# Keys and values of the attention heads: four full products replaced by seven block products

## What is computed

```python
h = rmsnorm(x, mix_norm_g[l])
u = h @ w_in[l]
ml_qk, ml_v, ml_o, ml_i, ml_f, mb_q, mb_k, mb_v = jnp.split(u, splits, axis=-1)
...
q_b = rmsnorm(heads(mb_q, Hb), q_norm_g[l]) * scale
k_b = rmsnorm(heads(mb_k, Hb), k_norm_g[l])
v_b = heads(mb_v, Hb)
h_b = moba_attention(q_b, k_b, v_b)
...
x = x + concat(h_m, h_b) @ w_out[l]
x = x + moe_ffn(rmsnorm(x, ffn_norm_g[l]), ...)        # 32 experts, 4 per token
x = x + sigmoid(rmsnorm(x) @ w_ple_gate[l]) * (p[l] @ w_ple_proj[l])
```

## Time and profile before

| | |
|---|---|
| Median of 3 runs | 1095.73 us (1095.69 to 1096.56) |
| Profiled execution, its own time | 1097.34 us |
| Span of the profiled execution, first to last instruction | 1095.5 us |
| Mean granted clock of TensorE | 0.995 |
| TensorE matmul busy | 1063.8 us (97%) |
| VectorE, ScalarE, GpSimd busy | 284.6, 146.9, 45.6 us |
| Bytes moved | 431.88 MB, mean 394 GB/s |

### The profile page before, as it was taken

One profiled execution on the slowest core, in us unless ns is written; L12 is line 12 of the kernel. 1 busy time (PEld: TensorE's weight loads), 2 busy tenths in 40 slices (PEclk: granted clock), 3 DMA queues, 4 the chain that ended last, 5 costly groups with the idle time before them and its releaser, 6 DMA issues.

```text
span 1095.5 us, 11997 instructions
## 1 busy us (share of the span) xinstructions
PE 1063.8 (97%) x5118; PEld 445.2 (41%) x5118; DVE 284.6 (26%) x547; ACT 146.9 (13%) x291; POOL 45.6 (4%) x59
## 2 busy tenths in 40 slices
PE   9999999999999999999998999898989899999998
PEld 5485563434343434343433333333333243534335
DVE  4286441232121212121211111121112011211126
ACT  4134350100000000000000000000000110000014
POOL 2422400000000000000000000000000000000000
PEclk9999999999999999999999999999999999999999
DMA  9942779999999999999999999999999999999991
GB/s 348 364 176 105 305 327 425 427 407 430 427 427 435 429 431 430 433 429 429 434 429 434 429 430 430 433 433 430 427 434 427 432 431 430 433 429 424 423 372 42
DMA packets 33788, 431.88 MB, mean 394 GB/s; under 512 B 5207, under 2 KB 5727, under 8 KB 16582
## 3 DMA queue, kind: packets, MB, share of 16 engines
q1 hardware_dynamic: 33520, 431.06, 93.4%
q10 hardware_dynamic: 214, 0.04, 0.0%
HBM read 430.04 MB, written 1.06 MB: 394 GB/s over the span
## 4 chain that ended last, share of the span: by engine, by line
PE 69%; DMA 29%; DVE 1%; issue 0%; ACT 0%; DVEq 0%; ACTq 0%
PE hu L1258 25%; DMA ring<-in_w_gate_up 23%; PE po L1288 15%; DMA ring<-in_w_down 6%; PE aux L1201 6%; PE hu L1053 3%; PE aux L1209 3%; PE hu L844 3%; PE hu L1250 2%; PE hu L850 2%; PE hu L887 1%; PE aux L1465 1%; PE hu L1080 1%; PE hu L860 1%; PE po L1265 1%; PE aux L1234 1%
## 5 line engine op out<-in xcount | busy, mean ns | idle before, releaser
L1258 PE MATMUL hu<-ring,num_xg 128*64 128x512 f32 x1920 | 435.3, 600 | 18.0 <-DMA ring<-in_w_gate_up 17.6
L1258 PEld LDWEIGHTS hu<-ring,num_xg 128*64 128x64 f32 x1920 | 131.9, 137 | 301.7 <-issue 271.3
L1288 PE MATMUL po<-ring,arena 128*64 128x512 f32 x976 | 217.5, 597 | 6.7 <-DMA ring<-in_w_down 6.7
L1880 DVE TENSOR_SCALAR arena<-hu 128x512 f32<-128x512 f32 x31 | 21.4, 692 | 427.8 <-PE hu L1258 427.8
L1288 PEld LDWEIGHTS po<-ring,arena 128*64 128x64 f32 x976 | 70.0, 138 | 149.3 <-issue 145.6
L1856 DVE TENSOR_TENSOR arena<-arena,aux 128x512 f32<-128x512 f32 x58 | 37.3, 684 | 133.1 <-PE aux L1209 121.3
L1201 PEld LDWEIGHTS aux<-num_xg,big 128*128 128x128 f32 x512 | 58.4, 192 | 13.0 <-issue 13.0
L1201 PE MATMUL aux<-num_xg,big 128*128 128x128 f32 x512 | 61.4, 278 | 0.0
L1869 DVE TENSOR_SCALAR arena<-iota_s,posm,gates 128x128 f32<-128x128 f32 x64 | 17.8, 342 | 118.3 <-PE po L1288 115.3
L2240 ACT ACTIVATE hu<-arena 128x512 f32<-128x512 f32 x31 | 18.6, 602 | 196.4 <-DVE arena L1880 196.4
L2256 ACT COPY arena<-po 128x512 f32<-128x512 f32 x16 | 9.4, 586 | 221.8 <-PE po L1278 221.8
(11 more groups left out here) (315 smaller groups left out, 707.6 us busy)
## 6 DMA issues: line engine op xcount, KB each, us to landing
ring<-in_w_gate_up SPq DMA_DIRECT2D x44, 4096.0 KB, 36.4
ring<-in_w_down SPq DMA_DIRECT2D x22, 4096.0 KB, 36.0
ring<-in_w_gate_up SPq DMA_DIRECT2D x37, 2048.0 KB, 15.1
ring<-in_w_down SPq DMA_DIRECT2D x14, 2048.0 KB, 16.5
ring<-in_w_in SPq DMA_DIRECT2D x6, 2048.0 KB, 16.2
ring<-in_w_down SPq DMA_DIRECT2D x8, 1024.0 KB, 33.2
ring<-in_w_gate_up SPq DMA_DIRECT2D x6, 1024.0 KB, 7.8
ring<-in_w_out SPq DMA_DIRECT2D x2, 2048.0 KB, 11.9
```

The lines of the kernel that those rows point to most:

```text
L1258: last = mm(hu[n * SLOTS:(n + 1) * SLOTS, 2 * e + b, :], rows_of[:, k, e * SLOTS:(e + 1) * SLOTS], features(w[:, o:o + D], n), start=first ...
L1288: last = mm(bank[n * SLOTS:(n + 1) * SLOTS, :], actT[:, f, h * SLOTS:(h + 1) * SLOTS], w[:, o:o + NB], start=(h == 0 and f == 0), stop=(h ...
L1880: v.tensor_scalar(glu, hu[:, 2 * e, :], LIMIT, None, ALU.min).then_inc(glu_ready, 1)
```

## The change

The keys and values of the moba half (chunks 1 and 2) are made together as the product of a 2x2 block matrix of tokens and a 2x2 block matrix of weights, with seven `product` calls in place of jobs 2 to 5 (eight times four `mm`). Three of the seven are on a plain block of tokens and a plain block of the value weights (called `vb_weights`). The sums of partial products (`lead_p`, `lead_q`, `lead_r` are PSUM banks) give values of tile 0, keys of tile 1, keys of tile 0 and values of tile 1. The second plain product, which finishes the values of tile 0, stands sixth, and the product that finishes the values of tile 1 last.

The four differences of weights `n1` to `n4` (128x2048) are made on VectorE, between the norms and the gate's chain. GpSimd makes `s1` and `s2` earlier, ahead of its wait for the gate's chain. Three copies of partial products are added on ScalarE. The key halves are sums on VectorE, written to `normed`, which has four places now in place of two; they come in the order tile 1, tile 0. SyncE issues the load of `CHUNK_WO_B` behind the small loads and `negbc`, in place of ahead of them. GpSimd's `t1` also waits for the third new product and its `t2` for the last one.

```diff
             pe.wait_ge(xs_ready, TT)
-            job(2)
+            pe.wait_ge(normed_ready, 1)
+            wait_chunk(pe, 1)
+            wait_chunk(pe, 2)
+            product(lead_p, token_block(0, 0), vb_weights(0), True, False).then_inc(lead_ps, 1)
+            pe.wait_ge(row_sums, 2)
+            pe.wait_ge(lead_step, 1)
+            product(lead_r, s1, n1, True, False).then_inc(lead_ps, 1)
+            pe.wait_ge(lead_step, 2)
+            pe.wait_ge(part_copied, 1)
+            product(lead_p, s2, n2, False, False).then_inc(lead_ps, 1)
             norm_transposes(0)
...
-            job(3)
+            pe.wait_ge(row_sums, 3)
+            pe.wait_ge(lead_step, 3)
+            pe.wait_ge(part_copied, 3)
+            product(lead_p, s3, n3, False, False).then_inc(lead_ps, 1)
             norm_transposes(1)
-            job(4)
+            pe.wait_ge(row_sums, 4)
+            product(lead_r, s4, kb_weights(1), False, True).then_inc(chunk_done, 1)
+            pe.wait_ge(normed_ready, 2)
+            product(lead_q, token_block(0, 1), vb_weights(1), True, True).then_inc(lead_ps, 1)
             norm_transposes(2)
             norm_transposes(3)
-            job(5)
+            pe.wait_ge(lead_step, 5)
+            product(lead_p, token_block(1, 1), n4, False, True).then_inc(chunk_done, 1)
...
+            wait_chunk(dve, 1)
+            wait_chunk(dve, 2)
+            v.tensor_tensor(n1, kb_weights(0), vb_weights(0), ALU.subtract).then_inc(lead_step, 1)
             dve.wait_ge(gate_act, 2)
             gate(v.tensor_tensor(flog, fpre, fln, ALU.subtract))
...
+            dve.wait_ge(chunk_done, 1)
+            dve.wait_ge(lead_step, 1)
+            v.tensor_tensor(n2, kb_weights(1), n1, ALU.subtract).then_inc(lead_step, 1)
+            normed_half(1)
+            v.tensor_tensor(n3, kb_weights(1), kb_weights(0), ALU.subtract).then_inc(lead_step, 1)
+            normed_transposed(0)
...
+            dve.wait_ge(lead_ps, 3)
+            dve.wait_ge(lead_step, 2)
+            v.tensor_tensor(n4, vb_weights(1), n2, ALU.subtract).then_inc(lead_step, 1)
+            dve.wait_ge(lead_ps, 4)
+            dve.wait_ge(part_copied, 2)
+            v.tensor_tensor(normed[:, 2, :], lead_p, lead_m5, ALU.add).then_inc(lead_step, 1)
+            normed_transposed(1)
+            normed_half(2)
+            dve.wait_ge(chunk_done, 2)
+            dve.wait_ge(part_copied, 3)
+            v.tensor_tensor(normed[:, 3, :], lead_r, lead_u2, ALU.add).then_inc(lead_step, 1)
+            normed_half(3)
+            normed_transposed(2)
             normed_transposed(3)
+            dve.wait_ge(part_copied, 1)
+            dve.wait_ge(lead_ps, 5)
+            v.tensor_tensor(vb[:, 0, :], vb[:, 0, :], lead_q, ALU.add).then_inc(vb_ready, 1)
...
             wait_chunk(pool, 5)
             wait_chunk(pool, 6)
+            pool.wait_ge(lead_ps, 3)
             g.tensor_tensor(t1, o_weights(0), v_weights(0), ALU.subtract).then_inc(weight_sums, 1)
             pool.wait_ge(weight_sums, 1)
             g.tensor_tensor(t3, o_weights(1), o_weights(0), ALU.subtract).then_inc(weight_sums, 1)
+            pool.wait_ge(chunk_done, 3)
             g.tensor_tensor(t2, o_weights(1), t1, ALU.subtract).then_inc(weight_sums, 1)
```

More of the change, by code:

```diff
@@ L305, in hybrid_layer @@
         og_ready = sem("og_ready")
+        lead_ps = sem("lead_ps")
+        lead_step = sem("lead_step")
         row_sums = sem("row_sums")
@@ L415, in hybrid_layer, with kb_weights, vb_weights @@
         t3 = o_weights(0)
+        LEAD_COPIES = 3
+        def kb_weights(half):
+            return slot(1, NB, K)[:, 4 * half:4 * half + 4, :]
+        def vb_weights(half):
+            return slot(2, NB, K)[:, 4 * half:4 * half + 4, :]
+        n1 = num_xg[:, 0:4 * NB].rearrange("p (k n) -> p k n", n=NB)
+        n2 = big1[:].rearrange("p (k n) -> p k n", n=NB)
+        n3, n4 = kb_weights(0), n2
+        lead_u2, lead_m5 = big2[:, 0:NB], big2[:, NB:2 * NB]
+        lead_p, lead_q, lead_r = hu[:, 0, :], hu[:, 1, :], po[:, 1, :]
         def wo_weights(half, n):
@@ L483, in wait_job @@
             else:
-                eng.wait_ge(job_ps, sum(not last_of_chunk(i) for i in range(j + 1)))
+                eng.wait_ge(job_ps, sum(not last_of_chunk(i) for i in range(j + 1) if i < 2 or i >= J_QK))
         def selections(pair):
@@ L566, in _ @@
                     sp.dma_start(brb[:], b_router.to_broadcast([P, E])).then_inc(late_loaded, 16)
-            load(CHUNK_WO_B, slot(CHUNK_WO_B, D, 4), w_out_k[:, 4:8, :])
             sp.wait_ge(gate_step, GATE_STEPS)
@@ L575, in _ @@
                          .to_broadcast([P, H * S])).then_inc(negbc_loaded, 16)
+            load(CHUNK_WO_B, slot(CHUNK_WO_B, D, 4), w_out_k[:, 4:8, :])
             load(CHUNK_WO_A, slot(CHUNK_WO_A, D, 4), w_out_k[:, 0:4, :])
@@ L839, in job @@
                     wait_chunk(pe, n)
-                if j < J_QK:
-                    tt = j % 2
-                    for k in range(K):
-                        last = mm(bank, hT[:, k, tt * P:(tt + 1) * P], slot(n, NB, K)[:, k, :],
-                                  start=(k == 0), stop=(k == K - 1))
-                else:
-                    ct = (j - J_QK) % 4
-                    for k in range(K):
-                        last = mm(bank[:, 0:S], slot(n, NB, K)[:, k, ct * P:(ct + 1) * P], hT[:, k, :],
-                                  start=(k == 0), stop=(k == K - 1))
+                ct = (j - J_QK) % 4
+                for k in range(K):
+                    last = mm(bank[:, 0:S], slot(n, NB, K)[:, k, ct * P:(ct + 1) * P], hT[:, k, :],
+                              start=(k == 0), stop=(k == K - 1))
                 done_job(j, last)
@@ L926, in _, with product @@
             done_job(1, raw_job(1, range(2, K)))
+            def product(bank, rows_of, weights, first, last):
+                for k in range(4):
+                    ins = mm(bank, rows_of[:, k, :], weights[:, k, :], start=(first and k == 0), stop=(last and k == 3),
+                             skip_group_check=True)
+                return ins
             def norm_transposes(i):
@@ L1047, in output_transposes @@
                 last.then_inc(hmT_ps, 1)
-            def product(bank, rows_of, weights, first, last):
-                for k in range(4):
-                    ins = mm(bank, rows_of[:, k, :], weights[:, k, :], start=(first and k == 0), stop=(last and k == 3),
-                             skip_group_check=True)
-                return ins
             sum_p, sum_q, sum_r = hu[:, 0, :], hu[:, 1, :], hu[:, 2, :]
@@ new lines, in _ @@
+            block_roots(0)
+            act.wait_ge(gate_step, 3)
+            a.activation(fln, fneg, ACT.Exp).then_inc(gate_act, 1)
+            act.wait_ge(gate_act, 1)
+            a.activation(fln, fln, ACT.Ln, bias=1.0).then_inc(gate_act, 1)
+            block_squares(1)
+            act.wait_ge(lead_ps, 1)
+            a.copy(vb[:, 0, :], lead_p).then_inc(part_copied, 1)
+            block_roots(1)
+            act.wait_ge(lead_ps, 2)
+            a.copy(lead_m5, lead_r).then_inc(part_copied, 1)
@@ L2076, in _ @@
+            act.wait_ge(lead_ps, 3)
+            a.copy(lead_u2, lead_p).then_inc(part_copied, 1)
             act.wait_ge(gcol_ps, 1)
             act.dma_start(negm_d, negm).then_inc(negm_stored, 16)
+            for i in range(2, 4):
+                block_squares(i)
+                block_roots(i)
             a.activation(emc[:].rearrange("p t h -> p (t h)"), hu[:, 3, 0:TT * H], ACT.Exp).then_inc(emc_ready, 1)
-            for tt in range(TT):
-                wait_job(act, J_VB + tt)
-                a.copy(vb[:, tt, :], hu[:, tt, :]).then_inc(vb_ready, 1)
+            act.wait_ge(chunk_done, 3)
@@ L2083, in moba_exp @@
+            a.copy(vb[:, 1, :], lead_p).then_inc(vb_ready, 1)
             def moba_exp(h):
```

67 lines of the change are left out of this document (28 added, 39 removed).

## The result

The changed kernel took 1098.37 us (median of 20 executions, 1096.35 to 1099.32), the kernel before 1096.54 us beside it (20 executions, 1095.46 to 1097.02). The ratio is 1.0018, 95% interval 1.0011 to 1.0024: 2.0 us slower by the ratio, 1.8 by the medians, just short of the 0.2% that I had called telling. The forecast was 1095.6 with a range to 1098.2, so the result lies outside it. Of the 2.8 us between forecast and result (rounded parts), 0.8 are the base (the three executions that I had gave 1095.73, the twenty give 1096.54), 1.8 the change, 0.1 the gain that I had forecast.

What follows compares the result with a forecast made beforehand. The expert stream was taken to run at the transfers' pace, starting when the front part lets it. The section's 2.9 us would be lost behind t2 except 0.1: 1095.73 - 0.1 = 1095.6 us, range 1094.2 to 1098.2.

Steps and rivals of the forecast that it cites:

- The section: TensorE's stretch from 24.37 to 54.13 us, forecast to end near 51.2 with seven products, 2.9 us earlier.
- a wait of some 0.5 before the fourth: TensorE's fourth product waits for n3, which GpSimd's s3 and s4 can hold: up to 0.8 us, taken as 0.5.
- just covered: Before TensorE's third product: n2 on VectorE ends at 31.0, product due at 31.25, covered by 0.2 us.
- the 3.00 us row: VectorE's earlier 128x2048 difference at 103.23 us, read as 0.85 waiting for GpSimd's sum and 2.2 work.
- query halves: Two VectorE sums forming halves for the second token tile, after n4, costed at 0.69 us each.
- The loss behind t2: After the section GpSimd's t2 holds VectorE's second scaling to 61.0 us; gain only 0.1 us; chance 0.44.
- The change does not move this: chunk 6 keeps its place in the queue behind the same bytes: GpSimd's sums at the scalings: t1 stays at 47.19 us, t2 at 56.25 to 60.78.
- The moved load of output weights is read only when the heads are done, so I take it at nothing: SyncE's load of CHUNK_WO_B, moved behind the small loads, costed at nothing.
- The clock: Rival: TensorE's clock falls in the new gap, jobs 8 and 9 lose 1.4 to 1.7 us: 1097.2; chance 0.30.
- The base: Whole kernel before the change: median of the runs 1095.73 us, from which the forecast subtracted 0.1.

Runs made afterwards that it cites:

- e3: Changed kernel with GpSimd's t2 waiting for VectorE's four scalings of heads 0 and 1: 1093.64 us, ratio 0.9975 to the kernel before.
- e10: Changed kernel with the four scalings of heads 0 and 1 on ScalarE in place of VectorE: 1093.48 us, ratio 0.9976 to the kernel before.
- e8: Changed kernel with the load of CHUNK_WO_B at its old place and t1 waiting for the last norm's scale: 1096.66 us, ratio 1.0002.
- e4: Kernel before with only the load of CHUNK_WO_B moved behind the small loads: 1097.56 us, ratio 1.0012.
- e5: Changed kernel with only the router weights' load moved behind the other small loads: 1099.47 us, ratio 1.0025 to the kernel before.
- e11: Changed kernel with the three small loads of biases issued behind the load of CHUNK_WO_B: 1096.93 us, ratio 1.0006 to the kernel before.
- e9: Changed kernel with t2 waiting for the four scalings, and s3 and s4 ahead of GpSimd's wait for the gate's chain: 1093.08 us, ratio 0.9969.

## Why the prediction was wrong

Its mechanism was right, one step and one weighing were not.

- **The section.** Forecast: last product over at 51.2 us, 2.9 us less, with a wait of some 0.5 before the fourth. Measured: scores at 51.43, and 2.4 us less from the section's start to its end. Some 0.3 us were lost before the third product, which the forecast had as just covered (it is due at 30.9 and starts at 31.17, behind `n2`), and 0.56 before the fourth. `n1` took 2.29 us (forecast 2.28), and `n3` 3.13: it began 0.98 us before GpSimd's `s4` (32.70 to 33.97) was over, as worked out for the 3.00 us row. The seven products do shorten the section, by 2.4 us. (The two sums on VectorE that the prediction calls query halves are the key halves; their price, 0.69 us each, was right.)
- **The loss behind t2.** Forecast: the first scaling let in between `t3` and `t2`, the second held to `t2`'s end, the gain gone. Measured so (54.93 to 62.12), and shown from several sides: put `t2` later (e3) or the scalings on ScalarE (e10), and job 8 starts 2.9 and 3.1 us earlier than in the earlier trace rows; leave both and mend only the landing (e8), and the wait of TensorE stays. The Trainium skill, SBUF — State Buffer, Who interferes with whom, calls the pair of ports an exclusive lock held for a whole instruction, where issue order decides who blocks; the runs agree, with the addition that of two instructions of VectorE that were waiting, one got in between two back-to-back sums of GpSimd and the next did not.
- **The step that failed: "The change does not move this: chunk 6 keeps its place in the queue behind the same bytes".** It kept its place, but what stands directly *behind* it counts too. `t1` started at 48.45 in place of the forecast 47.2, `t2` ended at 62.0 in place of 60.8, and because I had rightly put `t2` on the chain, all of it went to job 8. The same error stands in "The moved load of output weights is read only when the heads are done, so I take it at nothing": I asked who reads the moved load, and not whose landing it changes. e4 gives some 1.2 us to that edit alone (1.1 by the medians, 1.3 by the ratio of 1.0012, whose interval is 0.3 to 2.3), the largest term of the result, and with the load back and `t1` guarded (e8) the median is 1096.66 us, within the range.
- **The clock.** I had given it 0.30 and 1.4 to 1.7 us. It fell in the profiled execution, in e5 and in e8, though not in e11's (a wait of 2.32 us). Its size was too large for the profiled execution: slower rows in front of job 8 are partly covered by VectorE's convolution, which leaves 0.6 us in the profiled execution; e5 shows 2.5 when it also covers job 8 (0.42 and 2.10). The prediction had priced it on top of the loss behind `t2`, and so it came.
- **The base.** The median of three executions was 0.8 us below that of twenty. Without that the result would lie inside the range: that the forecast's range was missed is owed to both, while the slowdown itself is the landing and the clock.

## What to carry to other kernels

A gain on one engine ends at the next resource that others hold: before costing a faster stretch at its face value, look for the instruction behind it that waits for a port or a lock, and give the holder a wait in the same edit (e3: one line, from 1.0018 to 0.9975). When a load is moved in a queue, ask not only who reads it but which landing it stood behind: small loads behind a large one on whose landing the chain hangs cost 1.2 us here. Moving an operation out of one instruction's way can put it in another's: `s3` and `s4` left `n3` alone in e9 and held what stands ahead of `n1`. And a wait of TensorE that is free by itself may be followed by its lower clock.
